# Attention with every fp32 product split into three fp32r products, in a one-core hybrid attention / state-space layer

## What is computed

```python
qb = q.reshape(b, nb, Q_BLOCK, H_KV, rep, HD).transpose(1, 0, 2, 3, 4, 5)
scale = HD ** -0.5
def one_block(qi):
    s = jnp.einsum('bqgrd,btgd->bgrqt', qi, k, preferred_element_type=jnp.float32) * scale
    p = jax.nn.softmax(s, axis=-1).astype(v.dtype)
    return jnp.einsum('bgrqt,btgd->bqgrd', p, v)
```

## Time and profile before

| | us |
|---|---|
| median of 3 runs (lowest, highest) | 1858.96 (1855.09, 1859.84) |
| the profiled execution, and its span | 1860.62, 1858.9 |
| TensorE busy in the span | 1638.2 (88%) |
| VectorE busy | 1031.8 (56%) |
| ScalarE busy | 662.4 (36%) |
| mean granted TensorE clock | 0.936 of 2.4 GHz |
| TensorE's share of the chain that ended last | 72% |

### The profile page before, as it was taken

How to read it: one execution, slowest core, us unless ns; L and a number is a source line. 1 busy time by engine, 2 the same in 40 slices (tenths; PEclk the granted TensorE clock), 3 DMA queues, 4 the chain that set the end, 5 groups by cost and what they waited for, 6 DMA issues and landing times.

```text
span 1858.9 us, 27421 instructions
## 1 busy us (share of the span) xinstructions
PE 1638.2 (88%) x11141; PEld 1542.0 (83%) x11141; DVE 1031.8 (56%) x1419; ACT 662.4 (36%) x1099; POOL 99.5 (5%) x155
## 2 busy tenths in 40 slices
PE   4799999989998997888789899989289999999995
PEld 2699989889998987787755599989289999999995
DVE  5466675557754676786465353434934353342467
ACT  3544443334373265655455442321131121111210
POOL 1000012110101100000000000000000000000000
PEclk9799998999998999988899999999689999999998
DMA  9344355442486666664520164333102222223221
GB/s 306 98 128 139 126 172 195 131 136 65 153 268 235 211 208 222 179 205 163 181 106 23 46 199 148 115 139 112 45 24 69 70 74 71 79 68 90 68 68 56
DMA packets 159721, 241.14 MB, mean 130 GB/s; under 512 B 8048, under 2 KB 126560, under 8 KB 156576
## 3 DMA queue, kind: packets, MB, share of 16 engines
q1 hardware_dynamic: 136464, 171.45, 28.5%
q0 software_dynamic: 12304, 47.72, 6.9%
q10 hardware_dynamic: 10880, 20.97, 4.1%
HBM read 195.06 MB, written 45.06 MB: 129 GB/s over the span
## 4 chain that ended last, share of the span: by engine, by line
PE 72%; DVE 15%; ACT 7%; issue 3%; DMA 2%; SPq 0%; ACTq 0%; DVEq 0%
PE acc L805 64%; PE tp L805 5%; DVE arena L1850 2%; DVE wlo L1750 2%; ACT arena L1511 1%; ACT whi L1286 1%; PE tp L1190 1%; DVE arena L2003 1%; DMA arena<-in_w_mod 1%; PE tp L888 1%; DVE arena L1789 1%; DVE arena L1788 1%; ACT arena L1298 1%; DVE wlo L1801 1%; DVE arena L2005 1%
## 5 line engine op out<-in xcount | busy, mean ns | idle before, releaser
L805 PE MATMUL acc<-hh,whi 128*128 128x322 f32 x1408 | 343.3, 326 | 33.3 <-ACT arena L1298 20.1
L805 PE MATMUL acc<-hl,whi 128*128 128x322 f32 x1408 | 336.5, 321 | 0.0
L805 PE MATMUL acc<-hh,wlo 128*128 128x322 f32 x1408 | 333.2, 319 | 0.0
L805 PEld LDWEIGHTS acc<-hh,whi 128*128 128x128 f32 x1408 | 248.0, 199 | 37.1 <-ACT arena L1298 21.7
L805 PEld LDWEIGHTS acc<-hl,whi 128*128 128x128 f32 x1408 | 250.5, 198 | 0.0
L805 PEld LDWEIGHTS acc<-hh,wlo 128*128 128x128 f32 x1408 | 248.8, 197 | 0.0
L1286 ACT ACTIVATE whi<-raw 128x2048 fp32r<-128x2048 f32 x78 | 148.7, 1908 | 266.3 <-PE acc L805 266.3
L1750 DVE TENSOR_TENSOR wlo<-raw,whi 128x2048 fp32r<-128x2048 f32 x78 | 178.5, 2290 | 105.5 <-ACT whi L1286 105.2
L805 PE MATMUL acc<-whi,hh 128*128 128x256 f32 x720 | 207.6, 288 | 7.9 <-DVE hl L2238 7.9
L805 PE MATMUL acc<-whi,hl 128*128 128x256 f32 x720 | 204.3, 284 | 0.0
L805 PE MATMUL acc<-wlo,hh 128*128 128x256 f32 x720 | 204.1, 283 | 0.0
(11 more groups left out here) (255 smaller groups left out, 2331.3 us busy)
## 6 DMA issues: line engine op xcount, KB each, us to landing
raw<-in_w_in SPq DMA_DIRECT2D x38, 1024.0 KB, 7.0
raw<-in_w_mlp SPq DMA_DIRECT2D x32, 1024.0 KB, 5.4
arena<-in_w_mod SPq DMA_DIRECT2D x24, 1024.0 KB, 6.4
arena<-decay_sums_t ACTq DMA_DIRECT2D x40, 512.0 KB, 5.5
arena<-xs_nat SPq DMA_DIRECT2D x8, 1024.0 KB, 8.1
raw<-in_w_ssd_o SPq DMA_DIRECT2D x8, 1024.0 KB, 6.3
y_nat<-arena POOLq DMA_DIRECT2D x6, 1024.0 KB, 7.3
arena<-y_nat SPq DMA_DIRECT2D x6, 1024.0 KB, 5.9
```

The lines of the kernel that those rows point to most:

```text
L805: return pe.matmul(out, l, r, start=first, stop=last)
```

## The change

Every product of the attention is made of three fp32r products of upper and lower parts.

- Heads: ScalarE's copies out of PSUM write the upper part, VectorE subtracts (`heads_lower`), POOL stores both. The cached keys likewise.
- V and the cached V: ScalarE rounds the upper parts before `weights(F_END)`, VectorE subtracts behind its own.
- Loads: K, V and the cached upper keys are loaded during the last chunk; Q comes head by head into two buffers (`q_in`).
- Scores and values: `thrice`. The values product covers two steps (256 queries) and not a head; its output, upper and lower, is copied for two steps at a time.
- Three probability buffers. Normalising moves from VectorE to ScalarE (`probabilities` in ACT's program); VectorE only inverts the sum (`inverse_sums`).
- The transposed probabilities are copied out as an upper part by ScalarE (`probs_out`, which now signals `p_hi`) and a lower part by VectorE (`probs_lower`, which signals `p_copied`). In VectorE's step n the order is `maxima(n + 2)`, `inverse_sums(n + 1)`, `probs_lower(n - 1)`, then `att_lower`.
- Several one-off semaphores of the dt path are joined into three; their waits are the same.

The core of the diff, program by program (POOL, SP, PE, ACT, DVE):

```diff
             def heads_out(h0):
                 for h in (h0, h0 + 1):
                     po.wait_ge(copied["sem"], due(copied))
-                    po.dma_start(qkt_d[h], qts[:, h % 2]).then_inc(qo[h % 2]["sem"], step(qo[h % 2]))
+                    for n in range(2):
+                        po.dma_start(qkt_d[n, h], qts[:, h % 2, n].bitcast(F32)).then_inc(qo[h % 2]["sem"], step(qo[h % 2]))
...
+                    if c == NT - 1 and g == 2:
+                        sp.wait_ge(s["quad_ok"], 4 * (NT - 1))
+                        for o in pair("qts_out"):
+                            step(o, HQ + HKV)
+                            sp.wait_ge(o["sem"], value(o))
+                        sp.wait_ge(s["out_kv"], 48)
+                        for n, k in enumerate((kh, kl)):
+                            sp.dma_start(k[:].bitcast(F32), qkt_d[n, HQ:].rearrange("h p t -> p h t")).then_inc(s["att_in"], 16)
+                        sp.dma_start(kch[:].bitcast(F32).rearrange("p h t -> p (h t)"), kct_d[0]).then_inc(s["att_in"], 16)
+                        sp.dma_start(vn, v_d.rearrange("t p c -> p t c")).then_inc(s["av_in"], 16)
+                        sp.dma_start(vc, hk(a["cache_v"])).then_inc(s["av_in"], 16)
...
+            def q_in(h):
+                b = h % 2
+                if h >= 2:
+                    sp.wait_ge(s["score_ready"], 4 * (h - 1))
+                for n in range(2):
+                    sp.dma_start(qb[:, b, n].bitcast(F32), qkt_d[n, h][:, 0:LAT]).then_inc(qin[b]["sem"], step(qin[b]))
             sp.wait_ge(s["states_ready"], 4 * NT)
-            for c in pair("qts_out"):
-                step(c, (HQ + HKV) // 2)
-                sp.wait_ge(c["sem"], value(c))
-            sp.wait_ge(s["out_kv"], 48)
-            heads = qkt_d.rearrange("h p t -> p h t")
-            sp.dma_start(qT[:, HQ:], heads[:, HQ:]).then_inc(s["att_in"], 16)
-            sp.dma_start(qT[:, 0:2], heads[:, 0:2]).then_inc(s["att_in"], 16)
+            q_in(0)
             sp.wait_ge(s["fall_ok"], NT * NG)
-            sp.dma_start(kcT.rearrange("p h t -> p (h t)"), kct_d).then_inc(s["att_in"], 16)
-            sp.dma_start(vn, v_d.rearrange("t p c -> p t c")).then_inc(s["av_in"], 16)
-            sp.dma_start(vc, hk(a["cache_v"])).then_inc(s["av_in"], 16)
-            sp.dma_start(qT[:, 2:HQ], heads[:, 2:HQ]).then_inc(s["av_in"], 16)
+            sp.dma_start(kcl[:].bitcast(F32).rearrange("p h t -> p (h t)"), kct_d[1]).then_inc(s["att_in"], 16)
+            q_in(1)
...
+            def thrice(out, l, r, first=True, last=True):
+                mul(out, l[0], r[0], first, False)
+                mul(out, l[0], r[1], False, False)
+                return mul(out, l[1], r[0], False, last)
...
-                    q = qT[:, h, t * P:(t + 1) * P]
-                    mul(acc[:, 2 * u, 0:LAT], q, qT[:, HQ + h // R, 0:LAT])
-                    last = mul(acc[:, 2 * u + 1, 0:PAST], q, kcT[:, h // R])
+                    q = [qb[:, h % 2, i, t * P:(t + 1) * P] for i in range(2)]
+                    thrice(acc[:, 2 * u, 0:LAT], q, [k[:, h // R, 0:LAT] for k in (kh, kl)])
+                    last = thrice(acc[:, 2 * u + 1, 0:PAST], q, [k[:, h // R] for k in (kch, kcl)])
...
                 pe.wait_ge(prob["sem"], due(prob))
                 step(pt_free)
                 if some(pt_free, 1):
                     pe.wait_ge(pt_free["sem"], value(pt_free, 1))
                 for j in range(6 if n < N_SCORE else R):
-                    last = pe.transpose(tp[:, j // 4, (j % 4) * P:(j % 4 + 1) * P], pr[:, u, j * P:(j + 1) * P], ident)
+                    last = pe.transpose(tp[:, j // 4, (j % 4) * P:(j % 4 + 1) * P], pr[:, n % 3, j * P:(j + 1) * P], ident)
...
-                    for j in range(6):
-                        v = (vn[:, 1 + j] if j < 4 else vc[:, j - 4])[:, (h // R) * HD:(h // R + 1) * HD]
-                        last = mul(o, v, pT[:, h % 2, j], j == 0, j == 5)
+                if j == 0:
+                    pe.wait_ge(s["v_ok"], 2)
+                o = tp[:, 2 + j % 2]
+                if j < N_SCORE // 2:
+                    pe.wait_ge(s["p_copied"], 2 * (j + 1))
+                    c = slice(j // 2 // R * HD, (j // 2 // R + 1) * HD)
+                    for i in range(6):
+                        v = [vh[:, 1 + i, c], vl[:, 1 + i, c]] if i < 4 else [vch[:, i - 4, c], vcl[:, i - 4, c]]
+                        last = thrice(o[:, 0:2 * P], v, [pT[:, j % 2, b, i] for b in range(2)], i == 0, i == 5)
...
+                if n % 2 == 0 and n:
+                    values(n // 2 - 1)
+            for j in range(N_SCORE // 2, N_SCORE // 2 + HKV):
+                values(j)
...
+            act.wait_ge(s["av_in"], 32)
+            act.activation(vh[:], vn, ACT.Copy).then_inc(s["v_hi"], 1)
+            act.activation(vch[:], vc, ACT.Copy).then_inc(s["v_hi"], 1)
...
+            def probabilities(n):
+                w = n % 3
+                act.wait_ge(ex["sem"], n + 1)
+                act.wait_ge(sums["sem"], due(sums))
+                if n < N_SCORE:
+                    last = act.activation(pr[:, w], pr[:, w], ACT.Copy, scale=sm[:, w, 12:13])
+                else:
+                    for r in range(R):
+                        p = pr[:, w, r * P:(r + 1) * P]
+                        last = act.activation(p, p, ACT.Copy, scale=sm[:, w, 12 + r:13 + r])
+                last.then_inc(prob["sem"], step(prob))
...
-                probs_out(n)
-                if n % 4 == 1 and 4 < n < N_SCORE:
-                    att_out(n // 4 - 1)
+                if n:
+                    probs_out(n - 1)
+                probabilities(n)
+                if n % 2 == 1 and n > 2:
+                    att_out((n - 3) // 2)
                 if n - 1 in GATED:
                     q = GATED[n - 1]
                     squares(0, q, z0[:, q * 512:(q + 1) * 512])
-            att_out(HQ)
...
+            def heads_lower(n):
+                for h in range(2):
+                    dve.wait_ge(qhi["sem"], due(qhi))
+                    dve.tensor_tensor(qts[:, h, 1, LAT:], tp[:, 2 * h + 1, 0:P], qts[:, h, 0, LAT:].bitcast(F32), ALU.subtract)
+                    dve.tensor_tensor(qts[:, h, 1, 0:LAT], tp[:, 2 * h], qts[:, h, 0, 0:LAT].bitcast(F32),
+                                      ALU.subtract).then_inc(qlo["sem"], step(qlo))
...
+            dve.wait_ge(s["v_hi"], 1)
+            dve.tensor_tensor(vl[:], vn, vh[:].bitcast(F32), ALU.subtract).then_inc(s["v_ok"], 1)
+            dve.wait_ge(s["v_hi"], 2)
+            dve.tensor_tensor(vcl[:], vc, vch[:].bitcast(F32), ALU.subtract).then_inc(s["v_ok"], 1)
...
+            def inverse_sums(n):
+                w, k = n % 3, 1 if n < N_SCORE else R
                 dve.wait_ge(ex["sem"], due(ex))
+                dve.reciprocal(sm[:, w, 12:12 + k], sm[:, w, 4:4 + k]).then_inc(sums["sem"], step(sums))
+            def probs_lower(n):
...
+                dve.wait_ge(phi["sem"], due(phi))
                 if n < N_SCORE:
-                    do(dve.reciprocal(sm[:, u, 12:13], sm[:, u, 4:5]))
-                    dve.tensor_scalar(pr[:, u], pr[:, u], sm[:, u, 12:13], None, ALU.mult).then_inc(prob["sem"], step(prob))
+                    j, t = n // 2, n % 2
+                    hi_, lo_ = (pT[:, j % 2, b, :, t * P:(t + 1) * P] for b in range(2))
...
+                dve.tensor_tensor(lo_, src, hi_.bitcast(F32), ALU.subtract).then_inc(plo["sem"], step(plo))
...
             maxima(0)
             maxima(1)
+            inverse_sums(0)
             for n in range(N_SCORE + HKV):
-                probabilities(n)
                 if n + 2 < N_SCORE + HKV:
                     maxima(n + 2)
-                if n % 4 == 1 and 4 < n < N_SCORE:
-                    att_lower(n // 4 - 1)
+                if n + 1 < N_SCORE + HKV:
+                    inverse_sums(n + 1)
+                if n:
+                    probs_lower(n - 1)
+                if n % 2 == 1 and n > 2:
+                    att_lower((n - 3) // 2)
                 if n in GATED:
                     gated(0, GATED[n])
-            for h in range(HQ - 1, HQ + 2):
-                att_lower(h)
+            probs_lower(N_SCORE + HKV - 1)
+            for j in range(N_SCORE // 2, N_SCORE // 2 + HKV):
```

More of the change, by code:

```diff
@@ L18 @@
 NT = (CTX + LAT) // P
+NKC = PAST // P
 HQ, HKV, HD = 8, 2, 128
@@ L255, in build @@
         kmx = ysc[:, 0]
+        part = lambda n, at, *shape: nc.alloc_sbuf_tensor_at(n, [P, *shape], F32R, offset=A0 + 4 * at)
         c4 = Carve()
[L259 to L262, removed]
+        pr = c4(3, LAT + PAST)
+        vh, vcl = part("v_hi_t", c4.at, NT, HKV * HD), part("cached_v_lo", c4.at + NT * HKV * HD, NKC, HKV * HD)
+        assert c4.at + (NT + NKC) * HKV * HD <= 4096
+        qc = (part("context_q_hi", 4096 + DI, HQ, P), part("context_q_lo", 4096 + DI + HQ * P, HQ, P))
+        assert 4096 + DI + 2 * HQ * P <= c5x - DI
         c4.at = c5x - DI
-        pT = c4(2, (LAT + PAST) // P, LAT)
-        assert c4.at <= AR - 11 * 1024
```

(39 more changed lines are left out.)

219 lines of the change are left out of this document (115 added, 104 removed).

## The result

The changed kernel takes 1942.3 us (median of four runs, 1937.7 to 1947.1) against 1858.8 us. The ratio is 1.045, with a 95% interval of 1.042 to 1.048. The prediction was 1939, with a range of 1902 to 1968.

A forecast was written before the change was run, and what follows sets the result against it. The prediction took the attention to be bound by TensorE and its short waits on other engines; 46.7 + 24 + 2 + 2.1 + 0.4 + 4.8 = +80 us on 1860.62 gave 1940.6, as median 1939 us, range 1902 to 1968.

The forecast's parts named there:

- TensorE's own work: Attention: scores 1.035 us for 1.29, values 2.12 us after every two steps; a pair of steps falls from 6.49 to 5.51.
- The pause: Attention: TensorE waits 2.53 us in each step before the transposes for VectorE's lower part; a pair takes 10.57 us.
- The clock: Attention: TensorE's clock falls in about six of ten pairs of steps, 2.5 us each, +24 us; bounds 0 and +88.
- Context scores: Attention's context steps: fp32r matmuls with 128 columns, between 0 and +4 us, taken as +2 us.
- The stage as a whole: Whole attention stage: +46.7 us at the upper clock, +24 for clock falls, +2 for context scores.
- Ahead of the attention: Before the attention: +2.1 us for VectorE's part of V, +0.4 for ScalarE's, +4.8 in the projections.
- The term behind the projections: Gate transposes after the projections wait for VectorE's weight split and subtractions; pause 2.58 us becomes 5.4, +4.8 us with clock.
- V's lower part: Before the attention's first maximum: VectorE subtracts V's upper part after its last weight split, +2.1 us.
- the clock holds: Rival: in the attention the pauses cost no clock, 1913 us; chance 0.20.
- Not slower: Rival: in the attention the lower part is ready before it is asked for, 1852 us; chance 0.04.

## Why the prediction was right

The time and the sign came out, and the mechanism with them. By its own steps:

- *TensorE's own work.* Scores 1.02 and 1.13 us for 1.04 and values 2.19 for 2.12 at the upper clock, in the pair of steps from 987.09 to 997.48, each counted from its first matmul to the start that could follow its last. That the scores fit is in part luck: the slope of the two rates in the earlier trace rows gives 0.239 us for 512 columns, not 0.227, and so 1.07 for the scores. The products measured 0.227.
- *The pause.* It is put down to the instruction named. 2.53 us were priced; the profile calls 2.24 to 2.26 us idle. The two are not counted from the same point: the profile's idle time starts at the modelled end of the last matmul (990.79 + 0.28), the price at the end of its interval (990.79 + 0.11 = 990.90). From there to the transposes at 993.33 it is 2.43 us, in three parts: 0.21 to the reduction for 0.26, 1.14 to the subtraction for 1.26, and 1.08 from it to the transposes for 0.96 + 0.05. The 0.26 fits by luck: 943.71 in the earlier trace rows is where the weight load of the transposes began, which had itself waited for VectorE's normalising, and not the end of the scores. A pair of steps took 10.39 us (987.09 to 997.48, transposes to transposes) for 10.57, two pauses too dear by 0.1 us each.
- *The clock.* Falls in about ten of sixteen pairs at 2.5 us each were priced, +24. Of the 13 pairs between VectorE's maxima from 951 to 1101 us five were longer, by 3.0 us on average (13.07 to 14.38 us for 10.39), 15 us together. With 10.39 us a pair the stage would take 175.8 - 16 x 0.18 + 0.9 (context scores, below) = 173.8 us at the upper clock, so by this estimate some 20 us of it are the clock, the rest of them at its two ends. Fewer falls, each dearer, and bounds of 0 and +88 that were wide: the size is in part luck. The run with the pause filled shows that pauses of this length do cost clock when they come in every step: the granted clock is 0.93 for 0.86, and the stage shorter in spite of 38.6 us more work. The table of the Trainium skill (TensorE: Matmul & The Clock Gate, "Why this matters for your kernels") warns only of longer pauses; that shorter ones are free was my reading of it. The trace does not bear that reading out. But the row at 932 us, which I had called against the rule, is of a pause of 3.36 us, longer than the 2.5 in question, and so says little about them.
- *Context scores.* 12 products of 128 columns took 1.37 us (from 1110.09) and 1.28 us (from 1116.42). The four plain ones before, which the trace records as eight, took 0.89 us (from 1042.23): +0.9 in all for +2.
- *The stage as a whole.* +64.9 measured, 46.7 + 24 + 2 = 72.7 priced.
- *Ahead of the attention.* +7.1 for 2.1 + 0.4 + 4.8 = 7.3. The term behind the projections is well met: TensorE's pause there is 5.26 us for the 5.4 foreseen, and its distance to the kernel before grows by 5.2 us, from 2.15 to 7.34. V's lower part took 2.0 us for 2.1 (936.33 to 938.34). TensorE's next projection block starts at 513.75 in the chain of waits, behind a weight split, the two heads' lower parts and the gate transposes, in the order foreseen:

```profile
508.28 2.29 DVE wlo L1817
510.57 0.20 DVE qk_parts L2012
510.77 0.60 DVE qk_parts L2013
511.37 0.20 DVE qk_parts L2012
511.57 0.61 DVE qk_parts L2013
512.17 0.14 issue
512.31 0.58 PE tp L1019 x2
```

But the changed kernel was already 2.2 us late at 440 us, and between 590 and 908 us, in the scan, it won 3.8 us. I found no cause for either. The profiled executions of six kernels that are the same up to the attention (the changed one among them) have their first maximum anywhere from 931.6 to 943.7 us, at 936.3 in the mean. Four with the code of the kernel before up to there have it from 920.7 to 933.4, at 928.0 in the mean. So the agreement of the two executions is worth little. The means differ by 8.3 us, and the medians give 83.5 - 64.9 - 8.6 = 10 us for what lies ahead.
- *Not foreseen:* the 8.6 us behind the attention, 7.9 of them in the MLP's loop. The prediction looked at what each engine does and waits for, and not at the length of its program. That 1939 met 1942 is owed in part to this: the attention was priced 7.8 us too high and what lies behind it 8.6 too low.

Of the rivals, "the clock holds" was wrong (1913, and 0.86 in the stage). "Not slower" had the right condition: with the lower part ready before it is asked for, the stage came out at 119 us, shorter than before.

## What to carry to other kernels

In a software pipeline on in-order queues, nothing that waits for the newest product may stand in front of something that the oldest one still needs. Write down for each instruction which piece of TensorE's work it waits for, sort the queue by that, and do it for every engine: here VectorE's order was worth 38 us of a 194 us stage, and ScalarE's, together with the output's lower part half a step later, another 37. Price a pause at its own length and at the clock behind it; and when code is written out, look at the instruction queue's packets in the loops that follow.

## What the hardware showed that I had not expected

- A longer TensorE program costs in a loop that it did not touch: three pauses of 1.5 to 2 us and some 30 packets of instructions more, with 12250 instructions and more. At 11578 and fewer there were no pauses. Length and the place where the loop starts were not told apart.
- 416 needless products, 38.6 us more busy time of TensorE, made the changed kernel some 20 us faster (18.4 to 20.6), 11 of them seen in the stage.
- An fp32r product with 128 columns takes 0.11 us (12 in 1.28 and 1.37 us), hardly less than one with 256 (0.118).
- Pauses of 1.96 us between plain fp32 work left a clock of 0.79 in the stage, pauses of 2.24 us between fp32r work 0.86. Why the shorter ones cost more is open.
